# Storing the high and low halves of a transposed activation block by block instead of 8 KB apart

## The reference, cut to what matters

```python
def swiglu(h, w_in, w_out):
    gate, up = jnp.split(h @ w_in, 2, axis=-1)      # 1024 -> 2 x 2816
    return (jax.nn.silu(gate) * up) @ w_out         # 2816 -> 1024

x = x + FFN_HALF * swiglu(rmsnorm(x, ffn1_norm[l]), ffn1_w_in[l], ffn1_w_out[l])
```

## Time and profile before

| | us |
|---|---|
| median of 3 runs | 2495.45 |
| lowest and highest run | 2494.07, 2495.94 |
| the profiled execution | 2489.12 |
| its span, first to last instruction | 2487.3 |

### The profile page before, as it was taken

How to read it: one execution, slowest core, us unless ns; L and a number is a source line. 1 busy time by engine, 2 the same in 40 slices (tenths; PEclk the granted TensorE clock), 3 DMA queues, 4 the chain that set the end, 5 groups by cost and what they waited for, 6 DMA issues and landing times.

```text
span 2487.3 us, 40215 instructions
## 1 busy us (share of the span) xinstructions
PE 2373.2 (95%) x15724; PEld 2145.0 (86%) x15724; DVE 1096.1 (44%) x1913; ACT 1109.5 (45%) x1261; POOL 1703.8 (69%) x1340
## 2 busy tenths in 40 slices
PE   8999999998999999999999999999899999899997
PEld 7888889998988888898899898889788888788886
DVE  3335565423333333455553233333425764423766
ACT  4334434446433433444443644345445335455333
POOL 6997545545798898764445578985456986445985
PEclk9999999999999999999999999999899999999999
DMA  6554323333455565442323345564233555323553
GB/s 234 186 187 151 120 90 99 117 104 103 161 197 188 167 202 186 152 153 86 96 92 111 127 136 171 189 206 137 77 111 130 192 186 157 108 82 118 187 189 110
DMA packets 312206, 360.04 MB, mean 145 GB/s; under 512 B 18636, under 2 KB 291072, under 8 KB 311936
## 3 DMA queue, kind: packets, MB, share of 16 engines
q1 hardware_dynamic: 311866, 358.01, 44.4%
q10 hardware_dynamic: 198, 0.06, 0.0%
HBM read 357.00 MB, written 1.05 MB: 144 GB/s over the span
## 4 chain that ended last, share of the span: by engine, by line
PE 83%; DVE 9%; ACT 5%; issue 2%; POOL 1%; DMA 0%; ACTq 0%; DVEq 0%
PE ps L538 41%; PE ps L570 17%; PE ps L572 8%; PE ps L614 3%; PE ps L801 1%; POOL sb_lo L514 1%; PE ps L754 1%; PE ps L808 1%; PE ps L1065 1%; PE ps L1041 1%; DVE sb_vT L1765 1%; DVE sb_levels L1833 1%; PE ps L810 1%; PE ps L825 1%; ACT sb_hi L1162 1%
## 5 line engine op out<-in xcount | busy, mean ns | idle before, releaser
L514 POOL TENSOR_TENSOR sb_lo<-sb_raw,sb_hi 128x512 fp32r<-128x512 f32 (+1 forms) x1336 | 1703.6, 1309 | 760.7 <-ACT sb_hi L1162 759.9
L1162 ACT ACTIVATE sb_hi<-sb_raw 128x2048 fp32r<-128x2048 f32 (+3 forms) x341 | 639.7, 1877 | 689.5 <-PE ps L572 363.3
L570 PE MATMUL ps<-sb_hT,sb_hi 128*128 128x512 f32 x1792 | 635.0, 398 | 0.0
L538 PE MATMUL ps<-sb_hT,sb_hi 128*128 128x256 f32 (+1 forms) x2952 | 576.7, 288 | 18.7 <-DVE sb_qT L2024 5.3
L572 PE MATMUL ps<-sb_hT,sb_lo 128*128 128x256 f32 x1792 | 503.1, 281 | 0.0
L538 PEld LDWEIGHTS ps<-sb_hT,sb_hi 128*128 128x128 f32 (+1 forms) x2952 | 471.4, 191 | 28.9 <-issue 16.9
L538 PE MATMUL ps<-sb_hT,sb_lo 128*128 128x256 f32 (+1 forms) x1476 | 417.6, 283 | 0.0
L570 PEld LDWEIGHTS ps<-sb_hT,sb_hi 128*128 128x128 f32 x1792 | 336.7, 188 | 82.9
L572 PEld LDWEIGHTS ps<-sb_hT,sb_lo 128*128 128x128 f32 x1792 | 338.4, 189 | 2.1
L538 PE MATMUL ps<-sb_hi,sb_o_h 128*128 128x512 f32 (+1 forms) x848 | 306.2, 361 | 6.3 <-DVE sb_o_l L2110 3.0
L538 PE MATMUL ps<-sb_lo,sb_o_h 128*128 128x512 f32 (+1 forms) x848 | 301.8, 356 | 0.0
(11 more groups left out here) (343 smaller groups left out, 3041.7 us busy)
## 6 DMA issues: line engine op xcount, KB each, us to landing
sb_raw<-in_ffn_w_in SPq DMA_DIRECT2D x88, 1024.0 KB, 5.1
sb_raw<-in_w_in SPq DMA_DIRECT2D x78, 1024.0 KB, 5.2
sb_raw<-in_ffn_w_out SPq DMA_DIRECT2D x44, 1024.0 KB, 4.9
sb_raw<-in_ffn_w_up SPq DMA_DIRECT2D x44, 1024.0 KB, 5.1
sb_raw<-in_ffn_w_down SPq DMA_DIRECT2D x22, 1024.0 KB, 4.9
sb_raw<-in_w_out SPq DMA_DIRECT2D x16, 1024.0 KB, 5.1
sb_raw<-in_w_branch_a SPq DMA_DIRECT2D x8, 1024.0 KB, 6.4
sb_raw<-in_w_branch_b SPq DMA_DIRECT2D x8, 1024.0 KB, 5.0
```

What stands on the lines that cost most here:

```text
L514: ins = nc.gpsimd.tensor_tensor(lo[:, slot, c], raw[:, slot, c], hi[:, slot, c].bitcast(F32), ALU.subtract)
L538: ins = mm(dst, s, m, start=first and n == 0, stop=last and n == 3 * len(pairs) - 1)
L570: mm(ps[:, bank + i, :].rearrange("p (h n) -> p h n", h=2), wh[:, c, i * P:(i + 1) * P], hT_both[:, :, c, :], start=c == 0, stop=False, sk ...
L1162: fn(hi[:, slot, 0:width], raw[:, slot, 0:width], ACT.Copy).then_inc(hi_ready, 1)
```

## The change

`hT` gets its axes in another order, so that block c of the high part (256 columns) is followed at once by block c of the low part. The tensor has the same size and place. Line 570 then reads 512 columns that stand in one run, where it read two runs of 256 columns; the built instruction has one dimension fewer. The other matmuls that read `hT` keep their form, at other addresses. Where ACT or DVE writes or reads two or three blocks of one part in one instruction (lines 1351, 1894, 1691, 1692), these blocks are now 2 KB apart and no longer one run. No instruction, wait or transfer is added, removed or moved.

```diff
-        hT_both = sb("hT", [P, 2, KB, S], F32R)
-        hT_h, hT_l = (hT_both[:, i] for i in range(2))
+        hT_both = sb("hT", [P, KB, 2, S], F32R)
+        hT_h, hT_l = (hT_both[:, :, i, :] for i in range(2))
...
-                        mm(ps[:, bank + i, :].rearrange("p (h n) -> p h n", h=2), wh[:, c, i * P:(i + 1) * P], hT_both[:, :, c, :],
+                        mm(ps[:, bank + i, :].rearrange("p (h n) -> p h n", h=2), wh[:, c, i * P:(i + 1) * P], hT_both[:, c, :, :],
```

## The result

The changed kernel took 2499.37 us (median of 12 runs, 2496.09 to 2501.5) against 2495.4 us for the kernel before (12 runs, 2491.73 to 2496.63): a ratio of 1.0018, with a 95% interval of 1.0009 to 1.0026. The forecast of no change was wrong: the time lies inside the range, but the kernel became slower by 4 us. That is less than the 5 us which the prediction took for what a measurement can tell, and still more than these runs leave uncertain, since the interval ends at 1.0009. The time also lies just above the 2492 to 2499 us of the likeliest case. Its profiled execution took 2496.53 us, 7.4 us more than that of before.

The account below looks back on a forecast made before the run. The prediction took PE, busy for 95% of the span, to bound the kernel. Its terms summed to 0 against the profiled 2489.12 us; with the median 6.3 us above that, it forecast 2495.4 us, range 2483 to 2500 us.

Parts of the forecast that it names:

- the likeliest case: Whole kernel: no change within 0.2% (5 us), chance 0.70, its own range 2492 to 2499 us.
- Items 1 and 2: PE matmuls reading hT: line 570 in one run, 0 ns (bounds -23 to +12.9 us); lines 538, 572, 614, 0.
- The excess of 6.4 ns per pair: Matmul pairs of `wide`: 353 ns against 346.4 for hop-free parts; said to come from alternating narrow and wide matmuls.
- Items 3 and 4: Two-block writes, ACT line 1351 and DVE line 1894, 8 times each: 0 taken, upper bounds 2.8 and 2.1 us.
- Item 5: DVE lines 1691 and 1692, twice each: 0 taken; 2 x 0.4 = 0.8 us if the cast lost its faster way.
- items 3 to 5: Strided ACT and DVE writes, the cast and the subtraction: 0 taken, 5.7 us together at their bounds, giving 2501.2 us.
- The third one: Rival: strided ACT and DVE writes cost what separate instructions cost, 2501 us; chance 0.04, including other small losses past 5 us.
- The first two: Rivals on `wide` pairs: hop is the excess, 2484 us (0.15), stronger form 2472 (0.03); pattern settles slow, 2508 us (0.08).

Follow-up runs that it names:

- cast_joined: The changed kernel, but the three blocks of cn_h and of cn_l each stand in one run of 768 columns again; 2492.89 us, ratio 0.9997.
- cast_apart: The kernel before, but cn_h and cn_l are blocks 0, 2 and 4, so lines 1691 and 1692 see three runs; 2499.17 us, ratio 1.002.
- after_filled: The changed kernel with 24 transposes of a constant on PE while it waits for line 2024; 2498.75 us, ratio 1.0015.
- after_mul_first: The changed kernel with the product of line 2023 moved ahead of line 2017; 2498.4 us, ratio 1.0014.
- delay_half: The kernel before with an added DVE copy of 768 columns on 32 partitions ahead of line 2020; 2502.61 us in one run.
- delay_full: The kernel before with an added DVE copy of 1536 columns ahead of line 2020; 2503.23 us in one run.
- same_again: The kernel before once more, unchanged; 2494.0 us, ratio 1.0004.
- delay_small: The kernel before with an added DVE copy of 16 columns on 32 partitions ahead of line 2020; 2493.04 us in one run.
- before_mul_first: The kernel before with the product of line 2023 moved ahead of line 2017; 2492.49 us, ratio 0.9992.
- cast_four_blocks: The changed kernel, but the cast of line 1691 takes four blocks instead of three, the subtraction still three; 2493.8 us, ratio 0.9999.
- cast_two_and_one: The changed kernel with the cast of line 1691 as two instructions, of two blocks and of one; 2493.24 us, ratio 0.9994.

## Why the prediction was wrong, point by point

**Items 1 and 2, line 570 and the other matmuls: right.** The pitch of a pair, the slow start of `down` and the total busy time are unchanged, and cast_joined, which has all of this and not the slow cast, is at 0.9997. The excess of 6.4 ns per pair is not the hop's. What it is was not tried.

**Items 3 and 4, the writes of two blocks: right.** 597 and 692 ns before and after.

**Item 5, the cast and the subtraction: the step that failed, twice over.** First in the value. The bound of 2 x 0.4 us was worked out rightly, from the subtraction's 958 ns, and the cast came out at it, 953 ns. The value taken was 0, and I took it where I had no row for an odd number of blocks: the row that I leaned on for separated writes was ACT's, and no DVE write with a gap stood in the rows. The cast had a faster way to lose, its 0.73 ns per column in the earlier trace rows against 1.25 for the subtraction, and I noted this without asking what the faster way wants. Then in the path. I summed durations and did not ask who waits behind the cast. The chain from it to line 2024, for which PE stood still 2.65 us per mixer in the kernel before, was in the list of waits and in no part of the prediction. Nor did I see that this chain crosses POOL's pieces. With that, 0.39 us became 1.25 us per mixer and 2.5 us in all, three times the bound of item 5. The error is to take a bound on an instruction's duration for a bound on what its delay does. That the time lies inside the range, and under the 2501.2 us of items 3 to 5, is luck: items 3 and 4 put 4.9 us into that sum and cost nothing, and nothing in the range stood for a wait that grows.

Of two pages of the Trainium skill that bear on this, one would have given the value. The page "VectorE: DVE Perf Modes" of the Trainium skill, in What auto-detection actually checks, says that a copy or cast of one SBUF source goes two elements at a time if the outermost dimensions of source and destination are even, or odd and equal. By this rule the cast keeps its way with 768 against 768 columns, loses it with 768 against 3 blocks, and keeps it with 4 or 2: all four cases agree with 560, 953, 693 and 427 ns. The page "SBUF — State Buffer" of the Trainium skill, Who interferes with whom, says that a VectorE instruction with two SBUF inputs and a GpSimd instruction that reads SBUF exclude each other, and that the later one stands until the earlier is through. Line 2023's ends, 1.08 us behind POOL's in both traces, agree.

**The rivals.** The third one, that the strided writes cost what separate instructions cost, came true in one of its three places and for another reason; it had 0.04. The first two had 0.26 and are out: all pairs kept their pitch.

**The rest of the loss is open.** The waits explain 2.5 of some 4 us. What is above comes with a lower granted clock. A straight line through each kernel's runs, read at a granted clock of 0.985, gives:

| kernel | runs | mean us | mean clock | us at 0.985 |
|---|---|---|---|---|
| before (first job) | 29 | 2493.4 | 0.9859 | 2494.6 |
| cast_joined | 11 | 2493.4 | 0.9855 | 2494.0 |
| cast_apart | 12 | 2498.0 | 0.9840 | 2496.4 |
| changed | 12 | 2499.1 | 0.9831 | 2497.2 |
| after_filled | 12 | 2497.7 | 0.9846 | 2497.0 |
| after_mul_first | 12 | 2496.8 | 0.9847 | 2496.3 |

The slopes of these lines differ, 1.0 to 1.8 us for each 0.001, and the changed kernel was measured apart from the others, so the last column is good to about 1 us, which is an estimate. At equal clock the kernels with the slow cast are 1.7 to 2.6 us above, and the waits come to 2.5 us. Their clock is also lower, by 0.001 to 0.003, at some 1.4 us for each 0.001. In the profiles, a stretch at the lower level stands behind the first mixer's wait for line 2024 in all five kernels where it is 3.3 us or longer without filling (changed, cast_apart, delay_half, delay_full, after_mul_first), and in none of the five others read for it (before, same_again, cast_joined, delay_small, before_mul_first), where it is 2.65 us or shorter. In cast_four_blocks and cast_two_and_one (2.5 us) there is none either.

The second mixer does not bear this out. There the wait is followed by no such stretch in the changed kernel and in cast_apart, where it is 3.5 us, and it is followed by one in same_again, which is the kernel before itself with its 2.65 us, and in before_mul_first, cast_four_blocks and cast_two_and_one. The other three kernels with the longer wait have one there too. First the changed kernel, then same_again:

```profile
2149.90:2172.10 22.20, 15.86 (x102) 1.00 0.42 142
```

```profile
2149.30:2152.70 3.40, 2.99 (x14) 0.51 0.00 0
```

So a longer wait is neither needed for such a stretch nor enough for it, and one profile of each kernel cannot tell how often it brings one. Taking the first mixer's stretch away by filling did not bring the time back, and with three filled waits the changed kernel was still at a lower clock. Whether the longer waits cause the rest, or it comes from where later waits fall, is not shown.

## What to carry to other kernels

When a layout changes, go through every instruction that touches the tensor, and for a DVE copy or cast compare the numbers of blocks of source and destination: here three blocks against one run cost 70% more, and four did not. Then follow who waits behind that instruction to the matmul, with the other engine's pieces on the way: 0.39 us more on a chain with 0.38 us to spare cost 1.25 us, and 0.20 us cost nothing. And look at the granted clock behind PE's waits: 56 idle transposes per mixer in three waits of 2.5 to 3.6 us, which do nothing but keep PE at work, gave 0.4% of the whole kernel, where the layout gave nothing.

## What the runs showed of the hardware that I had not expected

- The hop of 8 KB within a moving operand of 512 fp32r columns is free: 353 ns per pair of matmuls with it and without it.
- The same cast of 768 columns takes 560 ns into one run and 953 ns into three blocks 2 KB apart; 1024 columns into four take 693 ns. A copy of 3 x 256 columns on 32 partitions took 0.94 us, one of 6 x 256 columns 0.95 us.
- DVE's two-input product and POOL's subtraction take turns. The product of 1024 columns took 1.22 us where POOL stood still, and 1.30, 1.37, 1.50 or 2.37 us by where it came between POOL's pieces of 1.26 to 1.30 us; the piece that came behind it in the kernel before took 2.25 us. A DVE copy on its faster way does the same: 0.95 us alone, 1.93 us behind a piece.
- Equal runs differ by up to 10 us (2487.6 to 2497.8 in 29 runs of one kernel), and most of it goes with the mean granted clock, 0.982 to 0.989, at about 1.4 us for each 0.001.
